# Feature-form weight pieces of a hybrid block kernel: products of 256 columns into one half of a bank, and an evacuation by VectorE alone

## The reference

```
h = x + RMSNorm_post(Mixer(RMSNorm_pre(x)))
y = h + RMSNorm_post(ConvFFN(RMSNorm_pre(h)))

Mixer:   proj = xn @ w_in        (2048 x 7184: q, k, v of 8 stick-breaking heads, q, k, v, z and
                                  two gates of 8 gated-DeltaNet heads)
         heads -> concatenated 2048 columns -> @ w_out (2048 x 2048)
ConvFFN: u = xn @ w_up           (2048 x 11264), causal depthwise convolution of width 3, bias
         gelu(gate half) * value half -> @ w_down (5632 x 2048)
RMSNorm: x * rsqrt(mean(x^2) + 1e-6) * gain
```

## Time and profile before

| | |
|---|---|
| median of 3 runs | 1225.43 us (1225.2 to 1225.55) |
| the profiled execution, its own time | 1225.67 us |
| its span in the trace | 1223.9 us |
| TensorE matmul busy | 1204.1 us (98%) |
| TensorE weight load busy | 1031.7 us (84%) |
| VectorE, ScalarE, GpSimd busy | 73%, 60%, 16% |
| granted TensorE clock | 0.998 of full speed |

### The profile page before, as it was taken

How to read it: one execution, slowest core, us unless ns; L and a number is a source line. 1 busy time by engine, 2 the same in 40 slices (tenths; PEclk the granted TensorE clock), 3 DMA queues, 4 the chain that set the end, 5 groups by cost and what they waited for, 6 DMA issues and landing times.

```text
span 1223.9 us, 19897 instructions
## 1 busy us (share of the span) xinstructions
PE 1204.1 (98%) x6499; PEld 1031.7 (84%) x6499; DVE 888.9 (73%) x1703; ACT 729.7 (60%) x1438; POOL 196.8 (16%) x242
## 2 busy tenths in 40 slices
PE   8999999999999999999999999999999999999997
PEld 5888898888888888888888888888888888888886
DVE  5889986875457556887887888888888875555554
ACT  6877466646786546756656656665665554454542
POOL 1131111010221000122222231232222210000000
PEclk9999999999999999999999999999999999999999
DMA  9646434643434553555555555545554565555541
GB/s 362 264 182 225 165 115 130 229 170 141 143 144 183 189 201 138 187 192 187 190 180 197 193 184 198 179 174 203 180 197 173 204 241 178 200 198 185 202 172 69
DMA packets 34885, 227.79 MB, mean 186 GB/s; under 512 B 5504, under 2 KB 5904, under 8 KB 8208
## 3 DMA queue, kind: packets, MB, share of 16 engines
q1 hardware_dynamic: 33536, 224.48, 51.0%
q10 hardware_dynamic: 1296, 2.61, 0.6%
HBM read 224.91 MB, written 2.17 MB: 186 GB/s over the span
## 4 chain that ended last, share of the span: by engine, by line
PE 86%; DVE 8%; ACT 3%; DMA 2%; issue 1%; SPq 0%; POOL 0%; DVEq 0%; ACTq 0%; POOLq 0%
PE bank L1424 32%; PE bank L1428 16%; PE bank L1450 10%; PE bank L1452 10%; PE bank L1451 10%; DVE w_lo L920 3%; DMA arena<-in_x_tok 2%; DVE arena L941 2%; ACT w_hi L478 1%; PE bank L1553 1%; PE bank L1703 1%; PE bank L1702 1%; PE bank L1701 1%; DVE arena L925 0%; PE bank L1537 0%
## 5 line engine op out<-in xcount | busy, mean ns | idle before, releaser
L920 DVE TENSOR_TENSOR w_lo<-raw,w_hi 128x512 fp32r<-128x512 f32 x816 | 567.8, 718 | 238.2 <-ACT w_hi L478 235.8
L478 ACT ACTIVATE w_hi<-raw 128x512 fp32r<-128x512 f32 x816 | 502.3, 630 | 357.8 <-PE bank L1424 184.3
L1424 PE MATMUL bank<-xhl,w_hi 128*128 128x512 f32 x2028 | 650.1, 398 | 6.0 <-DVE arena L925 4.1
L1428 PEld LDWEIGHTS bank<-xhl,w_lo 128*128 128x128 f32 x2028 | 381.3, 188 | 87.8
L1428 PE MATMUL bank<-xhl,w_lo 128*128 128x256 f32 x2028 | 398.8, 278 | 0.0
L1424 PEld LDWEIGHTS bank<-xhl,w_hi 128*128 128x128 f32 x2028 | 313.0, 189 | 8.2 <-DVE w_lo L920 5.9
L1452 PE MATMUL bank<-w_hi,ffn_act 128*128 128x512 f32 x336 | 130.7, 389 | 0.0
L1451 PE MATMUL bank<-w_lo,ffn_act 128*128 128x512 f32 x336 | 130.7, 389 | 0.0
L1450 PE MATMUL bank<-w_hi,ffn_act 128*128 128x512 f32 x336 | 130.7, 389 | 0.0
L445 POOL TENSOR_TENSOR arena<-arena,token_scale 128x256 f32<-128x256 f32 x88 | 78.6, 908 | 299.4 <-DVE arena L925 191.4
L1340 DVE SCALAR_TENSOR_TENSOR arena<-arena,fcw 128x256 f32<-128x256 f32 x176 | 85.3, 484 | 23.9 <-DVE arena L1340 1.5
(11 more groups left out here) (255 smaller groups left out, 962.6 us busy)
## 6 DMA issues: line engine op xcount, KB each, us to landing
raw<-in_wts SPq DMA_DIRECT2D x203, 1024.0 KB, 4.8
xfeat<-in_x SPq DMA_DIRECT2D x4, 512.0 KB, 10.0
arena<-in_x_tok SPq DMA_DIRECT2D x1, 2048.0 KB, 20.2
xfeat<-in_x_tok SPq DMA_DIRECT2D x1, 2048.0 KB, 9.2
out_y<-xfeat SPq DMA_DIRECT2D x8, 256.0 KB, 2.0
arena<-gate_rows SPq DMA_DIRECT2D x1, 1024.0 KB, 4.4
arena<-base_rows SPq DMA_DIRECT2D x4, 256.0 KB
arena<-in_post_gains ACTq DMA_DIRECT2D x1, 1024.0 KB, 4.8
```

The source lines that it names most:

```text
L478: nc.scalar.activation(w_hi[:, i % RING, :], raw[:, slot, quarter * PIECE:(quarter + 1) * PIECE], ACT.Copy).then_inc(hi_ready, 1)
L920: V.tensor_tensor(w_lo[:, i % RING, :], raw[:, slot, quarter * PIECE:(quarter + 1) * PIECE], w_hi[:, i % RING, :].bitcast(f32), ALU.subtra ...
L1424: return M(ps[j][:, :], w_hi[:, r % RING, kk * P:(kk + 1) * P], xhl[:, k, :, :].rearrange("p a t -> p (a t)"), start=(k == 0), stop=(k == ...
L1428: return M(ps[j][:, 0:T], w_lo[:, r % RING, kk * P:(kk + 1) * P], xhl[:, CHUNK_K * q + kk, 0, :], start=False, stop=False, skip_group_chec ...
```

## The change

In feature form the high product over (x_hi | x_lo) becomes two products of 256 columns, and all three products of a k-step add into the same 256 columns of the bank. They are issued in the order high, high, low. The half copy of ScalarE goes; VectorE reads the bank once and multiplies by the token scale in that instruction; GpSimd's multiplications go. Two places keep the old way in part: the first group of w_up (the token scale is not known yet when it is evacuated) keeps the 512-column product, ScalarE's copy, VectorE's sum and GpSimd's multiplication; and group 0 of w_in is copied by VectorE unscaled and multiplied by GpSimd. `halfs`, `first_added` and `first_halves` remain for that first group.

```diff
@@ GpSimd, w_up
             up_scale(UG)
-            with pool.Fori(0, UP_STEPS - 1) as i:
-                up_scale(i * 2 + (UG + 1))
+            with pool.Fori(0, UP_STEPS) as i:
                 act_lo(i)
-                up_scale(i * 2 + (UG + 2))
-            up_scale(UG + 2 * UP_STEPS - 1)
-            act_lo(UP_STEPS - 1)
@@ ScalarE, conv_first
-                act_e.wait_ge(s("scaled"), 4 * c + j + 1)
+                if c:
+                    act_e.wait_ge(bank_free, 4 * c + j + 5)
+                else:
+                    act_e.wait_ge(s("scaled"), j + 1)
@@ VectorE, evacuation
-            def added(n_, j, b, out_):
-                dve.wait_ge(half_ready, n_ + 1)
-                return V.tensor_tensor(out_, ps[b][:, 0:T], halfs[j % 4], ALU.add).then_inc(bank_free, 1)
+            def scaled(used, j, out_, row):
+                dve.wait_ge(piece_used, used)
+                V.tensor_tensor(out_, ps[j][:, 0:T], token_scale[:, row, :], ALU.mult).then_inc(bank_free, 1)
+
+            def feature_tile(g, j):
+                if g == 0:
+                    dve.wait_ge(piece_used, RING + 12 + j + 1)
+                    V.tensor_copy(proj[:, GROUP_TILE[0] + j, :], ps[j][:, 0:T]).then_inc(bank_free, 1)
+                    return
+                if g == 1 and j == 0:
+                    dve.wait_ge(s("x_scale"), 1)
+                scaled(16 * g + RING + 12 + j + 1, j, proj[:, GROUP_TILE[g] + j, :], 1 if 32 <= GROUP_TILE[g] < 40 else 0)
@@ VectorE, ffn_conv, and ahead of the w_up loop
-                dve.wait_ge(s("up_scaled"), i * 8 + (4 * part + q + 1))
+                dve.wait_ge(bank_free, (i * 2 + (UG + part)) * 4 + (q + 5 - SKIPPED))
...
+            dve.wait_ge(s("up_scaled"), GROUP)
             with dve.Fori(0, UP_STEPS - 1) as i:
@@ TensorE
-            def tile_piece(g, r, skipped, operand=None):
+            def tile_piece(g, r, skipped, wide=False):
...
-                for kk in range(0, CHUNK_K, 2):
-                    if operand is not None:
-                        operand(kk)
-                    high(kk)
-                    low(kk)
-                    low(kk + 1)
-                    last = high(kk + 1)
+                for kk in range(CHUNK_K):
+                    k, cols_ = CHUNK_K * q + kk, slice(kk * P, (kk + 1) * P)
+                    if wide:
+                        M(ps[j][:, :], w_hi[:, r % RING, cols_], xhl[:, k, :, :].rearrange("p a t -> p (a t)"),
+                          start=(k == 0), stop=False, skip_group_check=True)
+                    else:
+                        M(ps[j][:, 0:T], w_hi[:, r % RING, cols_], xhl[:, k, 0, :], start=(k == 0), stop=False,
+                          skip_group_check=True)
+                        M(ps[j][:, 0:T], w_hi[:, r % RING, cols_], xhl[:, k, 1, :], start=False, stop=False,
+                          skip_group_check=True)
+                    last = M(ps[j][:, 0:T], w_lo[:, r % RING, cols_], xhl[:, k, 0, :], start=False, stop=(k == KT - 1),
+                             skip_group_check=True)
                 last.then_inc(piece_used, 1)
```

More of the change, by code:

```diff
@@ L371, in follow @@
                     at[0] += 1
[L372 to L376, removed]
+                    j = at[0] - 13
+                    if 0 <= j < GROUP:
+                        pool.wait_ge(bank_free, j + 5)
+                        if j == 0:
                             pool.wait_ge(s("x_scale"), 1)
-                        tile = proj[:, GROUP_TILE[g] + j, :]
-                        query = 1 if 32 <= GROUP_TILE[g] < 40 else 0
-                        pool.tensor_tensor(tile, tile, token_scale[:, query, :], ALU.mult).then_inc(s("scaled"), 1)
+                        tile = proj[:, GROUP_TILE[0] + j, :]
+                        pool.tensor_tensor(tile, tile, token_scale[:, 0, :], ALU.mult).then_inc(s("scaled"), 1)
             def each(v):
@@ L479, in split, with first_halves @@
                                      ).then_inc(hi_ready, 1)
[L481 to L487, removed]
+            def first_halves(j):
+                act_e.wait_ge(piece_used, 16 * (IN_GROUPS + OUT_GROUPS) + RING + 12 + j + 1)
+                nc.scalar.activation(halfs[j], ps[j][:, T:2 * T], ACT.Copy).then_inc(half_ready, 1)
             def slots(g, a, b):
@@ L493, in slots @@
                         split(g, AHEAD + r)
-                    if r >= 13:
-                        group_halves(g, r - 13, SKIPPED)
+                    if r >= 13 and isinstance(g, int) and g == IN_GROUPS + OUT_GROUPS:
+                        first_halves(r - 13)
             act_e.dma_start(gains[:, :, :], pre_gains).then_inc(s("gains_in"), 16)
@@ L921, in split, with first_added @@
                                 w_hi[:, i % RING, :].bitcast(f32), ALU.subtract).then_inc(lo_ready, 1)
-            def added(n_, j, b, out_):
-                dve.wait_ge(half_ready, n_ + 1)
-                return V.tensor_tensor(out_, ps[b][:, 0:T], halfs[j % 4], ALU.add).then_inc(bank_free, 1)
+            def first_added(j):
+                dve.wait_ge(half_ready, j + 1)
+                V.tensor_tensor(fhist[:, j, 2:2 + T], ps[j][:, 0:T], halfs[j], ALU.add).then_inc(bank_free, 1)
+            def scaled(used, j, out_, row):
[9 more added lines that the diff above has]
+                scaled(16 * g + RING + 12 + j + 1, j, proj[:, GROUP_TILE[g] + j, :], 1 if 32 <= GROUP_TILE[g] < 40 else 0)
             V.memset(mark[:, 0:1], 0.0).then_inc(bank_free, 4)
@@ L953, in follow @@
                     if (p - 13) % 16 < GROUP and 13 <= p < 16 * FEAT_GROUPS + 1:
-                        g_, j = divmod(p - 13, 16)
-                        added(4 * g_ + j, j, j, proj[:, GROUP_TILE[g_] + j, :])
+                        feature_tile(*divmod(p - 13, 16))
                     if 1 <= g <= CONV_GROUPS and r in CONV_AT[g - 1]:
@@ L1318, in _ @@
                     split(UG, AHEAD + 12 + q)
-                added(UG * 4 + q - SKIPPED, q, q, fhist[:, q, 2:2 + T])
+                first_added(q)
             dve.wait_ge(s("h_sum"), 1)
@@ L1363, in up_group @@
                         split(g, AHEAD + 12 + q)
-                    added(g * 4 + (q - SKIPPED), q, q, fhist[:, q, 2:2 + T])
+                    scaled(g * 16 + (RING + 12 + q + 1), q, fhist[:, q, 2:2 + T], 0)
             V.memset(mark[:, 0:1], 0.0).then_inc(s("gelu_done"), 2)
@@ L1464, in first_piece @@
                     for k in (kk, kk + 1):
-                        M(ps[0][:, :], w_hi[:, 0, k * P:(k + 1) * P], xhl[:, k, :, :].rearrange("p a t -> p (a t)"),
-                          start=(k == 0), stop=False, skip_group_check=True)
+                        for a in range(2):
+                            M(ps[0][:, 0:T], w_hi[:, 0, k * P:(k + 1) * P], xhl[:, k, a, :],
+                              start=(k == 0 and a == 0), stop=False, skip_group_check=True)
                     pe.wait_ge(lo_ready, 1)
@@ L1667, in _ @@
             follow(SB_PLACE)
-            pe.wait_ge(s("scaled"), 4 * FEAT_GROUPS)
+            pe.wait_ge(bank_free, 4 * FEAT_GROUPS + 4)
             pe.wait_ge(s("o0_sb"), BATCHES)
@@ L1794, in _ @@
                     pe.wait_ge(s("hn_lo"), r + 4)
-                tile_piece(UG, r, SKIPPED)
+                tile_piece(UG, r, SKIPPED, True)
                 if r in (4, 7):
```

2 lines of the change are left out of this document (removed).

## The result

The changed kernel takes 1243.14 us (median of 4 runs, 1242.85 to 1243.31) against 1225.40 for the kernel before (4 runs): ratio 1.0145, 95% interval 1.0127 to 1.0162, 17.7 us slower. The forecast was 1232.2 us, 6.8 slower: the side and the range held, but the loss was 2.6 times the one forecast. The profiled execution took 1243.14 us, 17.5 more than the one before.

The account below looks back on a forecast made before the run. The prediction took TensorE's stream of products to bound the kernel: 1225.67 + 8.3 for narrower products - 1.5 for shorter waits = 1232.5 us, the median 0.24 lower at 1232.2; range 1215 to 1252.

Parts of the forecast that it names:

- What bounds the kernel: Whole kernel: a stream of products on TensorE; relief of other engines is worth only what TensorE now waits for them.
- Step 1: TensorE, w_in and w_up: three 256-column products at 117.5 ns each make a k-step 4.2 ns longer, 8.3 us lost.
- The second way to the same figure: w_up k-step: 8.4 ns beyond pure columns in two products, 4.2 each, added to 113.3 for 256 columns.
- A: Rival on 256-column products: distance 115 ns or less, k-step 345.0 ns, 8.1 us faster, 1217.3 us; chance 0.32.
- B: Rival on 256-column products: fixed cost per product, 120 to 121.7 ns, k-step 360 to 365, 1247 to 1257 us; chance 0.15.
- Steps 2 and 3: ScalarE drops 124 half copies, 48 us, beside TensorE's stream; VectorE's scaling evacuation costs the old 0.42 us; no gain.
- Steps 4 and 5: GpSimd loses about 111 us of multiplications; TensorE's three waits for an evacuated bank, 4.1 us, shrink by 1.5.
- The prediction's own sign: Wrong if the k-step falls below 348 ns, loads are missing, or TensorE's idle time moves by more than 4 us.
- Step 6: Ahead of the w_up loop: VectorE newly waits for GpSimd's four tiles, next split 3.5 us later; costs nothing, at most 3.5.

## Why the prediction was wrong in size

**What bounds the kernel**: right. TensorE was busy in all of the loop before and after, and its pace alone moved the loop.

**Step 1, the term that failed**: the distance x of 256-column products, put at 117.5 ns, measured 120.0. The k-step before is 348.3 ns, so a small error in x weighs heavily: three times 2.5 ns are 7.5 of the 11.7 ns by which a k-step grew, and the term should have been 11.7 x 1984 = 23.2 us instead of 8.3. The forecast took the middle between a pair of low products at 115 and the 120 towards which the earlier trace rows and the fixed cost pointed, and the 115 was the wrong reading. It is a distance of two starts, and in the same rows the high products stand at 235 where 512 columns take 226.6: what the low products seemed to save stood with the high ones. Single starts shift by some ns with what stands ahead; only sums over whole k-steps can be trusted. The second way to the same figure, 8.4 ns of excess in two products and so 4.2 in each, was a coincidence: the alternating order has 6.7 ns of excess in a whole k-step, just what one 256-column product costs in the changed stream, and leaves nothing for the 512-column one. The earlier trace rows could not decide: by the 112 ns of the later runs for short products, half of the products there at 112 and half at 120 give just its 116, which is an estimate after the fact. The rivals: A (115) is refuted; B (120 to 121.7) had the pace, but not the cause, and its 1247 us was too high because TensorE's idle time fell by 5.5 us and not by 1.5. No cost belongs to the product as such.

That the side was right is in part luck. The forecast of a loss came from taking the middle of two readings, one of them wrong, and A on the other side had a chance of 0.32.

The rule of the Trainium skill, page "TensorE: Matmul & The Clock Gate", section "Back-to-back issue gap", which it gives for a matmul in isolation, would as an estimate have 256 / 2.4 + 2.5 = 109.2 ns here; the measurement, 120.0 with full loads and 113.5 with half loads, decides against it for this stream. The load's 107 ns in its section "LDWEIGHTS (loading the stationary operand)" is near the 112 measured with 128 to 240 columns.

**Steps 2 and 3**: the evacuation is as costed. 4 copies are left, VectorE's evacuation takes 0.423 us instead of 0.421. Not foreseen: its splits took 690 ns for 718.

**Steps 4 and 5**: 1.5 us forecast, 2.0 measured alone. The size is near, the place was not: of that run's gain the three waits for a bank have 0.4, and the 1.3 us at line 1537 were not in the sum. The prediction's own sign, that it is wrong if TensorE's idle time moves by more than 4 us, came true: it fell by 5.5. Of the waits behind it the three banks have 1.6, the heads' operand 1.3, the low parts of pieces 1.0 and the first piece 1.8. With the three products alone it already fell by 3.2 (idle 16.6 of 1243.6 us), for which the forecast had no term.

**Step 6**: the wait came (2.93 us on VectorE; GpSimd, with VectorE standing still, took 2.63 us for 4.08) and cost TensorE nothing.

**The sum by the measured terms**: 23.2 us of pace (the matmuls' busy time rose by 23.0) less 5.5 of idle time is 17.7 us, against 17.7 between the medians and 17.5 between the two profiled executions. Against the forecast the pace was 14.9 us dearer and the waits 4.0 shorter, and that is the 10.9 us between 1232.2 and 1243.14. By the runs of single steps it is 20.7 (20.1 without the first w_up group) less 2.0, so 18.1, which is the same within their intervals. Where the pace is not paid in full is w_in. In the run with the three products alone the first product behind its feature form starts at 279.69 us for 276.24, 3.5 later where 7.5 were due. Most of the difference is waits of TensorE that became shorter: for the three banks 3.6 us for 4.1, for low parts of pieces 0.6 for 1.6, for the heads' operand 0.4 for 1.3, and ahead of the first piece 0.5 for 1.8. The last comes before any narrowed product, so it is not an effect of the pace, and no run explains it.

What stays open is the mechanism of the 6.7 ns: they appear with a full load (112 ns) behind 256 columns (113.3), are 4.7 behind 288, and are absent with smaller loads; behind 240 columns the load's 112 ns is all there is. No run shows what TensorE does in them.

## What to carry to other kernels

Cutting a wide product into narrower ones with the same total of columns is not free once a product is about as short as its weight load (113 and 112 ns here): 512 + 256 columns took 346.7 to 348.3 ns and 3 x 256 took 360. Relief of other engines is worth what the critical engine's waits say, here 2.0 us, and should not be paid for with more of the critical engine's time; look at every wait in the stretch, not only at those for the tile that the change touches. Judge a stream's pace by sums over a whole period: the distance of two starts can leave out what the next one pays.

## What the runs showed of the hardware

Three products in a row that add into the same 256 columns of a bank go at the pace of products into its two halves, 0.360 us a k-step in both. The order high, low, low, high is dearer than the alternating one, 348.3 for 346.7 ns a k-step. In the kernel before, VectorE's splits take 687 ns with GpSimd idle and 856 beside a busy GpSimd. In the run with 128-column products the granted clock did not stay up. TensorE was at its level of 2.4 GHz in the w_up loop, but in parts of w_in the granted clock went down to its level of 1.2 GHz (0.5 in the page's slices, 0.60 as the mean of 95 to 125 us), although it was busy throughout. Rows of that kernel (us, busy of each engine, clock):

```profile
PEclk9956999556999999999999999999999999999999
95.00:125.00 30.00, 30.00 (x168) 30.00 (x167) 15.41 (x29) 10.52 (x19) 0.00 (x0) 0.60 0.30 96
135.00:160.00 25.00, 25.00 (x227) 25.00 (x225) 24.30 (x65) 14.00 (x27) 0.00 (x0) 1.00 0.49 169
```

The runs with 192 and 240 columns had a clock of 0.993 and 0.994 over the whole span, this one 0.937. Its pace in the loop is that of the 192-column run, yet its first product of w_up comes at 540.2 us for 478.4. So the 61 us by which it is longer (1269.52 for 1208.27) were nearly all lost ahead of w_up, the part in which the clock was down at times. What brought the clock down was not tested.
